# Feed-forward way up of a streaming encoder as 2x2 block products in seven half-size products, way down in four parts

## What is computed

```python
D_FF = ((8 * D_MODEL // 3 + 255) // 256) * 256        # 2816
def _swiglu(u, w_up, w_down):
    a, b = jnp.split(u @ w_up, 2, axis=-1)
    return (jax.nn.silu(a) * b) @ w_down
...
u = _modulate(_rmsnorm(x, norm_g[l, 0]), ada[:, 0], ada[:, 1])
x = x + 0.5 * ada[:, 2][:, None, :] * _swiglu(u, w_ff1_up[l], w_ff1_down[l])
```

## Time and profile before

| | |
|---|---|
| median of 3 runs | 2007.68 us (2007.49 to 2008.88) |
| span of the profiled execution | 2006.3 us |
| its own time | no other time is given beside its span |
| TensorE busy | 1997.1 us |
| VectorE, ScalarE, GpSimd busy | 998.3, 570.6, 672.0 us |
| moved from and to memory | 264.75 MB |

### The profile page before, as it was taken

How to read it: one execution, slowest core, us unless ns; L and a number is a source line. 1 busy time by engine, 2 the same in 40 slices (tenths; PEclk the granted TensorE clock), 3 DMA queues, 4 the chain that set the end, 5 groups by cost and what they waited for, 6 DMA issues and landing times.

```text
span 2006.3 us, 24348 instructions
## 1 busy us (share of the span) xinstructions
PE 1997.1 (100%) x10051; PEld 1674.7 (83%) x10051; DVE 998.3 (50%) x1407; ACT 570.6 (28%) x837; POOL 672.0 (33%) x278
## 2 busy tenths in 40 slices
PE   9999999999999999999999999999999999999999
PEld 7888888987788888888898888889778898888888
DVE  4954266674465775311266634757643757311121
ACT  3221222334423422122232212224253233221221
POOL 1644334401000445444434544551200005543451
PEclk9999999999999999999999999999999999999999
DMA  9665366422234466333427645663222435423331
GB/s 300 206 213 171 86 199 207 103 74 84 63 96 135 127 183 215 84 100 105 131 77 208 201 134 147 170 204 73 84 74 64 124 108 158 121 80 99 90 113 66
DMA packets 352254, 264.75 MB, mean 132 GB/s; under 512 B 49998, under 2 KB 334338, under 8 KB 352144
## 3 DMA queue, kind: packets, MB, share of 16 engines
q1 hardware_dynamic: 350320, 262.63, 44.0%
q10 hardware_dynamic: 1536, 0.46, 0.1%
q0 software_dynamic: 288, 0.11, 0.0%
HBM read 261.07 MB, written 2.10 MB: 131 GB/s over the span
## 4 chain that ended last, share of the span: by engine, by line
PE 97%; DVE 1%; SPq 1%; DMA 1%; ACT 1%; issue 0%; ACTq 0%; DVEq 0%
PE bank L1550 28%; PE bank L1552 28%; PE bank L1551 28%; PE bank L1635 1%; PE bank L1636 1%; PE bank L1639 1%; PE bank L1577 1%; PE bank L1579 1%; PE bank L1578 1%; PE ps L1755 1%; DMA ada_block<-in_w_ada 1%; PE ps L1734 0%; PE ps L1743 0%; PE ps L1724 0%; SPq L559 0%
## 5 line engine op out<-in xcount | busy, mean ns | idle before, releaser
L668 POOL TENSOR_TENSOR w_lo<-stage,w_hi 128x1024 fp32r<-128x1024 f32 (+1 forms) x236 | 644.7, 2751 | 1164.8 <-ACT w_hi L728 1126.1
L1550 PE MATMUL bank<-u_hi,w_hi 128*128 128x512 f32 x1768 | 694.6, 393 | 0.4 <-DVE prod L1180 0.4
L1552 PE MATMUL bank<-u_hi,w_lo 128*128 128x512 f32 x1768 | 688.3, 389 | 0.0
L1551 PE MATMUL bank<-u_lo,w_hi 128*128 128x512 f32 x1768 | 688.0, 389 | 0.0
L728 ACT ACTIVATE w_hi<-stage 128x1024 fp32r<-128x1024 f32 (+2 forms) x335 | 348.4, 1073 | 553.5 <-DMA stage<-in_w_ff_up 302.9
L1550 PEld LDWEIGHTS bank<-u_hi,w_hi 128*128 128x128 f32 x1768 | 332.0, 188 | 72.2 <-issue 3.5
L1551 PEld LDWEIGHTS bank<-u_lo,w_hi 128*128 128x128 f32 x1768 | 332.1, 188 | 69.7 <-issue 1.9
L1552 PEld LDWEIGHTS bank<-u_hi,w_lo 128*128 128x128 f32 x1768 | 331.9, 188 | 69.6
L1550 PE MATMUL bank<-h_hi,w_hi 128*128 128x512 f32 x744 | 289.6, 389 | 0.1
L1551 PE MATMUL bank<-h_lo,w_hi 128*128 128x512 f32 x744 | 289.4, 389 | 0.0
L1552 PE MATMUL bank<-h_hi,w_lo 128*128 128x512 f32 x744 | 289.4, 389 | 0.0
(11 more groups left out here) (218 smaller groups left out, 1435.6 us busy)
## 6 DMA issues: line engine op xcount, KB each, us to landing
stage<-in_w_ff_up SPq DMA_DIRECT2D x172, 512.0 KB
ada_stage<-in_w_ada SPq DMA_DIRECT2D x128, 512.0 KB, 5.5
stage<-in_w_ff_down SPq DMA_DIRECT2D x32, 1408.0 KB
stage<-in_w_in SPq DMA_DIRECT2D x16, 1024.0 KB
ada_block<-in_w_ada SPq DMA_DIRECT2D x8, 1024.0 KB, 11.8
stage<-in_w_out SPq DMA_DIRECT2D x8, 1024.0 KB
stage<-in_w_in SPq DMA_DIRECT2D x40, 128.0 KB
stage<-in_w_in SPq DMA_DIRECT2D x10, 512.0 KB
```

The source lines that it names most:

```text
L668: nc.gpsimd.tensor_tensor(stage_tile(w_lo, kind, n), t, hi_tile(n, depth(kind, n)), ALU.subtract).then_inc(lo_ready, 1)
L1550: mm(bank[n % BANKS][:, :], hi[:, k, :], rhs_hi(k), start=(k == order[0]), stop=False)
L1551: mm(bank[n % BANKS][:, :], hi[:, k, :], rhs_lo(k), start=False, stop=False)
L1552: last = mm(bank[n % BANKS][:, :], lo[:, k, :], rhs_hi(k), start=False, stop=(k == order[-1]))
```

## The change

**Way up.** For all pairs but the first four (first feed-forward) or three (the others), the gate and value tiles (two output halves) by the two halves of the input channels make a 2x2 block matrix A; the two halves of the input channels by the two halves of the frames make a 2x2 matrix of activations. The product is formed by the Winograd form of Strassen's scheme in seven products of 4 column blocks by 256 frames (`part`, w = 1 to 7). VectorE forms four sums of weight blocks for each pair (`sum_blocks`: S3, S1, S2, S4), ScalarE rounds the blocks in five steps, GpSimd makes the remainders of A1 (A11 and A12), S1, A22 and S4, VectorE that of S2 and S3 (`low_23`). Three results are copied out of PSUM by ScalarE (`keep_p1`, `keep_u2`, `keep_p5`) and joined by VectorE (`gate_sum`, `value_sum`, `product`). ScalarE now makes `h_hi` (`round_h`). Sums of activations (T) are made once per feed-forward (`t_sums`, `t4_sum`).

**Way down.** Four parts (5, 5, 5 and 7 blocks deep) instead of two of 11; `h` is a ring of 7 blocks.

**Memory.** `stage` slots are 8 blocks deep instead of 11; `w_hi` holds 7 tiles as 14 half-tiles; places of most buffers change; `xs` has a place for each half of the frames. Modulation pieces get other points in the order (`piece_points`).

The core of the diff:

```diff
-HALF_FT = D_FF // P // 2
+KH = KT // 2
+PAIRS = D_FF // P
-STAGE_W = HALF_FT * 2 * P
-HI_W = HALF_FT * P
+STAGE_W = KT * 2 * P
+HI_SLOTS, HI_W = 7, KT * P
+RUN_ENDS = (5, 10, 15, 21)
+PART_AT = (0, 5, 10, 15, PAIRS)
+def first_pair(e):
+    return 4 if e == 0 else 3
+def ff_order(e):
+    order = [("U", n) for n in range(2 * first_pair(e))]
+    for p, run in enumerate(runs(e)):
+        for j in run:
+            again = j > run[0]
+            order += [(j, 1), (j, 2)] + [(j - 1, 4)] * again + [(j, 6), (j, 5)] + [(j - 1, 3)] * again + [(j, 7)]
+        end = run[-1]
+        order += [(end, 3)] + ([("D", p, 0), (end, 4)] if p < PARTS - 1 else [(end, 4), ("D", p, 0)])
+        order += [("D", p, m) for m in range(1, KT)]
+    return order
...
+def piece_points(e):
+    pairs = [[(j, 0) for j in range(RUN_ENDS[p] + 1, RUN_ENDS[p + 1] + 1)] for p in range(PARTS - 1)]
+    down = [[("D", p, m) for m in range(KT)] for p in range(PARTS)]
+    if e == 0:
+        return ([("U", 6), ("U", 7), (4, 0), (5, 0)] + [("D", 0, 0)] * 4 + down[0][1:] + pairs[0]
+                + sorted(down[1] + [("D", 1, 2), ("D", 1, 5)]) + pairs[1] + sorted(down[2] + [("D", 2, 2), ("D", 2, 5)])
+                + pairs[2] + down[3][:5])
+    if e % 3 == 0:
+        return (sorted(down[0] + [("D", 0, 2), ("D", 0, 5)]) + pairs[0] + sorted(down[1] + [("D", 1, 2), ("D", 1, 5)]) + pairs[1]
+                + sorted(down[2] + [("D", 2, 2), ("D", 2, 5)]) + [(16, 0), (18, 0), (20, 0)]
+                + down[3][:5])
+    return down[0] + down[1] + down[2]
...
         @block.sync
+            def slot_free(e, load):
...
+                if item in PAIR_NUMBERS:
+                    return done(e, ("U", 2 * item + 1) if item < first_pair(e) else (item, 4))
+                return done(e, ("D", item[1], 2 * item[2] + 1))
...
         @block.gpsimd
+            def low_block(e, j, step):
+                pool.wait_ge(hi_ready, hi_done(e, (j, step)))
+                pool.wait_ge(sums_ready, SUMS * (seven(e, j) + 1))
...
+                nc.gpsimd.tensor_tensor(lo, raw, hi, ALU.subtract).then_inc(lo_ready, 1)
...
         @block.scalar
+            def pair(e, p, j, run):
+                f, again, last = first_pair(e), j > run[0], j == run[-1]
...
+                if again:
+                    gate_late(e, j - 1)
...
+                elif j >= run[0] + 2:
+                    round_h(e, j - 2)
...
+                    round_block(e, j + 1, "A1")
+                    keep_p1(e, j)
+                    round_block(e, j + 1, "S1")
+                    round_block(e, j + 1, "S23")
+                    if again:
+                        gate_early(e, j - 1)
+                    round_block(e, j + 1, "A22")
+                    keep_u2(e, j)
+                    keep_p5(e, j)
+                    round_block(e, j + 1, "S4")
...
         @block.vector
+            def sum_blocks(e, j):
...
+                nc.vector.tensor_tensor(s[:, KH:KT, :], a[:, 0:KH, :], a21, ALU.subtract).then_inc(sums_ready, 1)
+                dve.wait_ge(sums_ready, SUMS * n + 1)
+                nc.vector.tensor_tensor(a21, a21, a22, ALU.add).then_inc(sums_ready, 1)
+                dve.wait_ge(sums_ready, SUMS * n + 2)
+                nc.vector.tensor_tensor(s[:, 0:KH, :], a21, a[:, 0:KH, :], ALU.subtract).then_inc(sums_ready, 1)
+                dve.wait_ge(sums_ready, SUMS * n + 3)
+                nc.vector.tensor_tensor(s4[n % 3][:, :, :], a[:, KH:KT, :], s[:, 0:KH, :], ALU.subtract).then_inc(sums_ready, 1)
+            def low_23(e, j):
+                n = seven(e, j) % 2
+                dve.wait_ge(hi_ready, hi_done(e, (j, "S23")))
+                dve.wait_ge(sums_ready, SUMS * (seven(e, j) + 1))
+                nc.vector.tensor_tensor(s23_lo[n][:, :, :], s23[n][:, :, :], block_hi(j, "S2", 2), ALU.subtract
+                                        ).then_inc(lo23_ready, 1)
+            def gate_sum(e, j):
+                dve.wait_ge(tile_done, done(e, (j, 7)))
...
+                nc.vector.tensor_tensor(c22[:, j % 2, :], alpha(j)[:, 0:FH], p5[:, j % 2, :], ALU.add).then_inc(c22_ready, 1)
+            def value_sum(e, j):
+                dve.wait_ge(tile_done, done(e, (j, 3)))
+                both = p1u2[:, j % 2, :]
+                nc.vector.tensor_tensor(both, both, beta(j)[:, :], ALU.add).then_inc(b_ready, 1)
+            def product(e, j):
...
+                nc.vector.tensor_tensor(prod[:, j % 2, :], silu[:, j % 2, :], p1u2[:, j % 2, :], ALU.mult).then_inc(product_ready, 1)
+            def pair(e, j, run):
+                f, again, last = first_pair(e), j > run[0], j == run[-1]
+                if again:
+                    gate_sum(e, j - 1)
...
+                elif j >= run[0] + 2:
+                    low_h(e, j - 2)
+                if not last:
+                    sum_blocks(e, j + 1)
...
+                pieces(e, (j, 0))
+                if not last:
+                    low_23(e, j + 1)
+                if again:
+                    value_sum(e, j - 1)
+                    product(e, j - 1)
...
         @block.tensor
+            def part_ready(e, j, w):
+                n, f = seven(e, j), first_pair(e)
...
+                elif w == 4:
+                    pe.wait_ge(c22_ready, n + 1)
+                elif w == 6:
+                    pe.wait_ge(copied, 3 * n + 1)
+                elif w == 7:
+                    pe.wait_ge(copied, 3 * n + 2)
...
+            def part(e, j, w):
...
+                weights_ready(e, j, w)
+                part_ready(e, j, w)
+                for k in range(KH):
+                    mm(dst, hi[:, k, :], r_hi_[:, k, :], start=(k == 0 and w < 3), stop=False, skip_group_check=True)
+                    mm(dst, hi[:, k, :], r_lo_[:, k, :], start=False, stop=False, skip_group_check=True)
+                    last = mm(dst, lo[:, k, :], r_hi_[:, k, :], start=False, stop=(k == KH - 1), skip_group_check=True)
+                last.then_inc(tile_done, 1)
```

More of the change, by code:

```diff
@@ new lines, with runs, run_of, part_of @@
+HI_STEPS = ("A1", "S1", "S23", "A22", "S4")
+LO_STEPS = ("A1", "S1", "A22", "S4")
+PAIR_NUMBERS = range(PAIRS)
+SUMS = 4
+def first_pair(e):
+    return 4 if e == 0 else 3
+def runs(e):
+    starts = (first_pair(e),) + tuple(end + 1 for end in RUN_ENDS[:-1])
+    return [range(a, end + 1) for a, end in zip(starts, RUN_ENDS)]
+def run_of(j):
+    return next(p for p, end in enumerate(RUN_ENDS) if j <= end)
+def part_of(j):
+    return next(p for p in range(PARTS) if j < PART_AT[p + 1])
+def ff_order(e):
[8 more added lines that the diff above has]
+    return order
@@ new lines, in prep_order @@
+def prep_order(e, steps):
+    order = [("U", n) for n in range(2 * first_pair(e))]
+    for p, run in enumerate(runs(e)):
+        order += [(j, step) for j in run for step in steps] + [("D", p, m) for m in range(KT)]
+    return order
+FF_ITEMS = []
+for _p, _end in enumerate(RUN_ENDS):
+    FF_ITEMS += list(range(RUN_ENDS[_p - 1] + 1 if _p else 0, _end + 1)) + [("D", _p, d) for d in range(KT // 2)]
+ITEM_AT = {item: n for n, item in enumerate(FF_ITEMS)}
+ORDER_AT = {e: {key: n for n, key in enumerate(ff_order(e))} for e in range(STAGES) if e % 3 != 1}
@@ new lines, in hi_tile, with block_hi, gate_half, value @@
+        def hi_tile(e, key):
+            first = hi_slot(e, key) * KT
+            return w_hi[:, first:first + depth(e, key), :]
+        def block_hi(j, name, blocks=1):
+            n = ODD_BLOCKS.index(name) if j % 2 else 7 + EVEN_BLOCKS.index(name)
+            return w_hi[:, n * KH:(n + blocks) * KH, :]
+        def gate_half(t, e, j, half):
+            return raw_slot(t, e, ITEM_AT[j])[:, half * KH:(half + 1) * KH, 0:P]
+        def value(t, e, j):
+            return raw_slot(t, e, ITEM_AT[j])[:, :, P:2 * P]
@@ new lines, in down @@
+            def down(e, p, end):
+                final, after = p == PARTS - 1, e + 1 < STAGES
+                for m in range(KT):
+                    if final and after and m == KT - 1:
+                        square(e + 1, KT - 1)
+                    if m == 0:
+                        gate_late(e, end)
+                        round_h(e, end - 1)
+                        if final:
+                            gate_early(e, end)
+                    if m == 1 and not final:
+                        gate_early(e, end)
+                    if m + AHEAD < KT:
+                        round_weights(e, ("D", p, m + AHEAD))
+                    elif not final:
+                        for step in (("A1",), ("S1", "S23"), ("A22", "S4"))[m + AHEAD - KT]:
+                            round_block(e, end + 1, step)
+                    elif after:
+                        round_weights(e + 1, first_tile(e + 1, m + AHEAD - KT))
+                    if m == (0 if final else 2):
+                        round_h(e, end)
+                    if e == 0 and p == 0 and m == 4:
@@ L935, in _ @@
                     round_u(l, 0)
-                for half in range(2):
-                    ff_half(l, 0, half)
```

(40 more changed lines are left out.)

1076 lines of the change are left out of this document (709 added, 367 removed).

## The result

The changed kernel takes 2195.07 us (median of 4 runs, 2188.25 to 2199.72) against 2008.04 on the same chip: a ratio of 1.093, 95% interval 1.091 to 1.0949. It is slower by 187 us, where the prediction said slower by 24 and its range ended at 2075. The sign was right, and the size was wrong by a factor of eight.

The account below looks back on a forecast made before the run. TensorE, holding 97% of the chain, was taken to bound the kernel. 2006.3 - 60 - 1.3 + 62 + 15 + 4 + 4 = 2030 us of span, plus 1.4: 2031.4 us, 1.2% slower; range 1975 to 2075.

Parts of the forecast that it names:

- TensorE's work, -61 us: On TensorE: 75 pairs as seven products save 0.80 us each, -60 us; shallower closing tiles of the way down, -1.3 us.
- The cycle and the pair stalls, +62 us: Pairs wait on a VectorE and GpSimd cycle of 11.0 us, 12.0 with a modulation piece, against TensorE's 10.08: +62 us.
- The lock: A VectorE operation with both inputs in SBUF and a GpSimd residual exclude each other for a whole instruction.
- lock absorbed: Rival: both engines interleave without gaps, pairs at 10.4 and 11.4 us, mostly eaten by slack; 1993 us, chance 0.25.
- no contention: Rival: no VectorE and GpSimd contention that matters, only ends and T sums remain; 1954 us, chance 0.06.
- The signs it named: Pairs at 11 or 12 us, TensorE waits before product 7 and A1, stretched VectorE operations, GpSimd over 60% busy.
- The ways down, +15 us: In six parts carrying 8 to 11 pieces, VectorE sums the next pair's blocks 2.5 us late (0 to 5): +15 us.
- the SP queue comes late: Rival: late VectorE delays weights queued with pieces, eight us more in each of six loaded parts; 2080 us, chance 0.14.
- Ends and T sums, +8 us: Four feed-forward ends, +4 us (0 to 8), and VectorE's sums for the T matrices, +4 us (0 to 10).
- the +4 us: At four feed-forward ends, six column blocks cover 2.2 us of the 4.1 between sum of squares and spread: +4 us.

Follow-up runs that it names:

- experiment 1: Changed kernel with GpSimd's residuals of a pair's blocks cut to 16 of 128 columns and TensorE taking the rounded part instead; 2102.63 us.
- experiment 11: Kernel of experiment 5 with the next pair's sums ahead of pieces on VectorE and ScalarE's copy of product 6 first; 2009.23 us.
- experiment 2: Changed kernel with rounded S2 and S3 copied to PSUM by ScalarE, so VectorE's low_23 reads them there in two halves; 2174.68 us.
- experiment 4: Kernel of experiment 1 with modulation pieces 2 to 8 of each vector also accumulating only 32 of 1,024 columns; 2072.36 us.
- experiment 5: Kernel of experiment 4 with the transfers of pieces 2 to 8 also cut, to 16 KB for 512 KB; 2053.97 us.
- experiment 6: Changed kernel with 638 matmuls into a bank nobody reads there, filling TensorE's longest stalls; 2178.71 us.
- experiment 10: Changed kernel with experiment 2's edit, next pair's sums ahead of pieces, product 6's copy first, and unread matmuls in its 20 longest stalls; 2133.98 us, ratio 1.0634.

## Why the prediction was wrong

**TensorE's work, -61 us: right.** Experiments 1 and 11 show the pace of 0.120 us and the saving. The Trainium skill's 109 ns would have promised 89 us; the rows of before decided rightly.

**The cycle and the pair stalls, +62 us: right.** 11.1 and 12.0 us were measured for 11.0 and 12.0, and 69 us over all. That the totals lie so close is partly luck: one step of 17.1 us in the first feed-forward, where the summing up of a vector stands between the sums and low_23, and last steps of 12.6 and 13.7 us in the third and last stages add some 11 us that the cycle doesn't hold, and the shorter last steps of other runs (9.5 to 9.9) take some off. The lock is shown by experiments 1 and 2; the rivals "lock absorbed" and "no contention" are out. The prediction read the exclusion in the earlier trace rows, as one of operations with both inputs in SBUF; but the h_hi cast there has one input and was stretched too (2.63 us, where the median of its line in the trace of before is 0.436), so that reading was too narrow. No term hung on it, since ScalarE now makes h_hi. For two SBUF inputs it is also the rule in SBUF — State Buffer of the Trainium skill ("Who interferes with whom"), and the trace agrees in both directions: low_23 at 2.82 us beside GpSimd, 0.68 a half with one input in PSUM. The signs it named are there: GpSimd busy over 60% in a quiet stretch (49.99 of 79.7 us), waits for keep_u2 ahead of product 7, means of VectorE's residuals far over their own length. The wait ahead of product 1 (A1) came in two kinds: 17 end with GpSimd's residual, as named (22.7 us), and 8 with ScalarE's rounding, which the prediction hadn't named (32.9 us).

**The ways down, +15 us: the step that failed.** "I take these 2.5 us late. Six parts: +15 us; 0 to 5 each is the range." Measured are 118 us in twelve parts: 81.6 in the six of the two heavy stages (13.6 each), 27 in the three of the third stage, which carries eight pieces in each and which the step didn't count, and 9.5 in the three without pieces. The step listed VectorE's work, never set it against the time there is, and guessed at the lateness. From c22 to c22 VectorE was busy for 40.7 to 48.6 us in each of the six, where TensorE needs 37.3: 16.8 to 20.6 us of pieces (the step had "over 12"), 2.8 to 7.6 of summing up vectors, and the locked operations stretched. It waited for pieces' transfers besides, 19 us in the six together. The block sums, ScalarE's roundings, GpSimd's residuals and TensorE's next run stand behind VectorE, so a late sum is the head of a line. Taking things away in turn shows what the 118 us were: 35 go with GpSimd's residuals (experiment 1), 21 with the pieces' arithmetic (4), 24 with their bytes (5), 15 with the order on VectorE and ScalarE (11), and 22 remain.

**The rival "the SP queue comes late"** was given 0.14 and 48 us. It was right that the queue has a part, but its mechanism, a late VectorE that delays the next weights, isn't what the traces show. ScalarE waited for weights of the way up for 1.5 to 3.4 us in each of the nine crossings with pieces, and for 1.5 to 2.2 in the three without, so these came hardly later for the pieces' sake. What VectorE waited for were the pieces, 28 us in the nine, and they stand behind the weights. Of the whole 187 us, taking things away in turn gave 92 us for GpSimd's residuals, 30 more for the pieces' arithmetic, 18 for their bytes, and 45 for the order on VectorE and ScalarE; in another order the shares might differ. What SyncE's waits for VectorE cost is not shown.

**The clock: missing.** No row of before has a granted clock other than 1.00, since TensorE never waited over 1.1 us, and no term of the sum had a price for its falling. It stretched the work by 45 to 55 us, by the width of the windows. That isn't its price, though: experiments 6 and 10 gave back 16 and 3.

**Ends and T sums, +8 us.** From the norm's spread to the first c22 the last stage took 53.7 us, and 48.2 in experiment 11; over four stages the difference is 29 us. The T sums, with both inputs in SBUF, are stretched by GpSimd's residuals (four narrow sums 5.95 us, where others took 1.66), and the first pair's products wait 3.04 and 3.38 us. At the ends TensorE waits for the norm's spread three times, 5.6 us in all and up to 2.6 at once, where it never waited for it before: the +4 us were near.

Pairs 69, crossings 118, starts 29 are 216 of the 249 us. The other 33 lie in the stages' starts and ends, most of them in experiment 11 too. I haven't taken them apart. Nor was it tried whether pieces sent by another queue, so that they stand behind no weights, would end VectorE's waits for them; the experiments show that fewer bytes alone don't.

## What to carry to other kernels

A saving on the bounding engine is bought with work on the others; here 61 us of TensorE's time were bought with 571 us of VectorE's, and the place to look is not their busy share over the span (72% for VectorE) but the densest stretch, where VectorE's work alone was longer than TensorE's. Write down each engine's queue for one such stretch, with its DMA waits and who stands behind whom, before pricing a step "late by some microseconds". And when an engine that was never idle becomes idle at all, ask for the clock it returns with.

## What was not expected of the hardware

The granted clock falls to half after stalls of a few microseconds: 8.29 us of idle time were followed by work at 1.2 GHz from 1238.76 to about 1244.6. Not every stall does it. Of three like stalls of 2.03 us in the last stage, ahead of 1918.28, 2001.60 and 2085.19, only the second shows it:

```profile
1916.00:1926.00 10.00, 7.97 (x67) 7.79 (x66) 9.40 (x8) 5.38 (x11) 8.02 (x4) 1.00 0.04 8
1999.00:2009.00 10.00, 7.97 (x54) 7.79 (x53) 9.30 (x8) 5.54 (x10) 7.99 (x4) 0.83 0.00 0
2083.00:2093.00 10.00, 7.96 (x67) 7.84 (x66) 9.41 (x8) 5.38 (x11) 8.02 (x4) 1.00 0.04 10
```

A transfer of 16 KB lands late behind large ones in its queue: the one of experiment 5 took 4.9 us behind 1 MB of weights, and the quickest of this size 1.6. The Trainium skill (DMA: Bandwidth & Descriptors, "Queues, rings and completion order") has each of the 16 engines take a queue's descriptors in order, and the trace agrees.

A VectorE subtraction of 512 columns with one input in PSUM ran 56 times wholly inside a GpSimd residual and never took over 0.69 us; one of 1,024 columns with both inputs in SBUF took up to 3.43 beside them, where 1.21 is its shortest.
